# Two 64-token blocks of one expert done together, weight chunk by weight chunk, in the rare path of a mixture-of-experts kernel

## The reference, cut to what matters

```
def moe_ffn(h, ...):                       # h: 256 x 1024, 32 experts, the best 4 of each token
    top_v, top_i = lax.top_k(logits, 4); gates = softmax(top_v)
    # for each expert e and the tokens xb sent to it:
    u = xb @ w_mlp1[e] + b_mlp1[e]         # 1024 x 2048
    x_glu = minimum(u[..., ::2], 7); x_lin = clip(u[..., 1::2], -7, 7)
    a = x_glu * sigmoid(1.702 * x_glu) * (x_lin + 1)
    y = a @ w_mlp2[e] + b_mlp2[e]          # 1024 x 1024
    # each token: sum of gate * y over its 4 experts
```

## Time and profile before

| | us |
|---|---|
| median of 3 runs | 1716.1 (1715.84 to 1716.47) |
| the profiled execution | 1711.69 |
| its span, first to last instruction | 1709.9 |
| PE busy | 1612.0 (94%) |
| PE matmuls of the experts' first layer, usual path | 461.7 in 2048 records |
| PE matmuls of their second layer | 243.3 in 1088 records |
| DMA, mean over the span | 319 GB/s |

### The profile page before, as it was taken

The page is one execution under the profiler, slowest core; times in us unless marked ns, Lnnn a source line. Parts: engine busy times, 40 slices in busy tenths (PEclk is TensorE's granted clock), DMA queues, the critical chain, the costliest instruction groups (busy, mean ns, idle before and its releaser), DMA issues.

```text
span 1709.9 us, 18899 instructions
## 1 busy us (share of the span) xinstructions
PE 1612.0 (94%) x7649; PEld 911.7 (53%) x7650; DVE 584.0 (34%) x930; ACT 472.9 (28%) x810; POOL 120.8 (7%) x222
## 2 busy tenths in 40 slices
PE   4999988999999999789999999989999999999998
PEld 2767334343343323334344333327888887788886
DVE  2666111111111101111011110117664667666654
ACT  3543110010011101001011010116554565455543
POOL 2001110110111101010011100000000000000000
PEclk9999998899999999899999999999999999999999
DMA  8988992799999999969999999996555544455540
GB/s 331 408 324 337 382 425 112 316 427 427 426 427 426 428 426 428 401 252 426 427 427 427 426 427 427 427 427 236 189 181 195 174 148 148 197 195 187 176 169 25
DMA packets 76304, 545.58 MB, mean 319 GB/s; under 512 B 8592, under 2 KB 8976, under 8 KB 10528
## 3 DMA queue, kind: packets, MB, share of 16 engines
q1 hardware_dynamic: 75744, 542.95, 78.0%
q10 hardware_dynamic: 448, 1.11, 0.2%
HBM read 542.98 MB, written 1.05 MB: 318 GB/s over the span
## 4 chain that ended last, share of the span: by engine, by line
PE 78%; DMA 16%; DVE 2%; issue 1%; ACT 1%; PEldq 1%; POOL 0%; SPq 0%; DVEq 0%; POOLq 0%; ACTq 0%
PE bank L274 75%; DMA slot<-w_mlp 15%; PE bank L278 3%; DMA h<-x 1%; PEldq L86 0%; DMA slot<-w_in_tail 0%; POOL mg L284 0%; ACT sq L281 0%; DVE XL L284 0%; ACT whf L281 0%; DVE h L292 0%; DVE u_l L292 0%; DVE u_g L288 0%; DVE u_s L284 0%; DVE tmp L284 0%
## 5 line engine op out<-in xcount | busy, mean ns | idle before, releaser
L274 PE MATMUL bank<-slot,xt 128*64 128x512 f32 x2048 | 461.7, 605 | 20.0 <-DMA slot<-w_mlp 19.9
L274 PEld LDWEIGHTS bank<-slot,xt 128*64 128x64 f32 x2048 | 143.6, 139 | 321.5 <-issue 272.8
L274 PE MATMUL bank<-slot,at 128*64 128x512 f32 x1088 | 243.3, 600 | 2.9 <-ACT at L281 2.9
L274 PE MATMUL bank<-wht,XH 128*128 128x512 f32 x528 | 207.7, 398 | 2.5 <-DVE XL L284 1.5
L274 PE MATMUL bank<-wlt,XH 128*128 128x512 f32 x528 | 204.3, 392 | 0.0
L292 DVE SCALAR_TENSOR_TENSOR wlt<-slot,colt,wht 128x512 fp32r<-128x512 f32 x248 | 177.4, 760 | 78.8 <-ACT wht L281 78.6
L274 PE MATMUL bank<-wht,XL 128*128 128x512 f32 x528 | 204.0, 391 | 0.0
L281 ACT ACTIVATE wht<-slot,colt 128x512 fp32r<-128x512 f32 x248 | 164.4, 718 | 91.9 <-PE bank L274 91.9
L288 DVE TENSOR_SCALAR u_g<-bank 128x512 f32<-128x512 f32 x34 | 23.5, 692 | 470.1 <-PE bank L274 470.1
L274 PEld LDWEIGHTS bank<-slot,at 128*64 128x64 f32 x1088 | 77.3, 138 | 154.0 <-issue 154.0
L281 ACT ACTIVATE u_s<-u_g 128x512 f32<-128x512 f32 x34 | 21.4, 630 | 498.2 <-DVE u_g L288 498.2
(11 more groups left out here) (314 smaller groups left out, 1528.4 us busy)
## 6 DMA issues: line engine op xcount, KB each, us to landing
slot<-w_mlp SPq DMA_DIRECT2D x384, 1024.0 KB, 25.5
slot<-gu SPq DMA_DIRECT2D x44, 1024.0 KB, 4.8
slot<-w_ada SPq DMA_DIRECT2D x24, 1024.0 KB, 10.2
slot<-down SPq DMA_DIRECT2D x22, 1024.0 KB, 4.7
slot<-w_in SPq DMA_DIRECT2D x18, 1024.0 KB, 5.0
slot<-w_out SPq DMA_DIRECT2D x8, 1024.0 KB, 7.5
slot<-w_gate SPq DMA_DIRECT2D x8, 1024.0 KB, 4.8
slot<-w_br_a SPq DMA_DIRECT2D x2, 1024.0 KB, 4.8
```

What stands on the lines that cost most here:

```text
L274: return pe(lambda e: e.matmul(o, l, r, start=start, stop=stop), *after, **kw)
```

## The change

An expert with more than 64 tokens no longer does one block and then the usual code. It takes a body of its own that does both blocks and then goes back to behind the whole usual code of that expert; the usual code is what the others run in line. In that body `first` and `second` take a list of blocks (`parts`), go through the weights once, and alternate between the blocks every two matmuls; the last block's last matmul on a chunk releases it. The second block has banks of its own (`FX`, `FY`, those of the other parity). The two `swiglu`s follow each other, since they share `u_g`, `u_s` and `u_l`. The checks for more than 128 and 192 tokens now come first in the body. For odd experts the `beside` work comes at the end of the body. `first_weights` moves from inside expert 0 to behind it.

```
-def seldom(kind, queues, far_sems, ap, bound, tag, body):
+def seldom(queues, far_sems, ap, bound, tag, body):
...
+def either(queues, sems, far_sems, ap, bound, tag, near, far):
...
+        q.items.append(("either", tag, ap, bound, usual, path, s.h, s.n - n))
...
+        at_x = nc.alloc_sbuf_tensor_at("at_x", [128, 4, 128], F32, offset=place["xt_x"][0])
...
+        def first(e, parts, release):
+            for X, Y, sel_, _, t_sel_, _, _ in parts:
+                for g, bk in enumerate((X, Y)):
+                    mm(bank[bk][:, :], sel_, brow[:, 512 * g : 512 * g + 512], True, False, t_sel_, T["brow"], *free[bk])
+            steps = first_early(e, range(4))
+            for two in zip(steps[0::2], steps[1::2]):
+                for i, (X, Y, _, x_of, _, t_x_, s_) in enumerate(parts):
+                    for k, j in two:
...
+                        if j == 3 and release:
+                            end_ = {"sem": rel, "sig": last_}
...
+        def gather_far(e, n, b0, *after):
...
             for b in range(2):
-                t = tr(bank[2][0:64, b * 128 : b * 128 + 128], ow_x[:, b, :], t_w, *free[2], sig=b == 1)
+                t = tr(bank[b0][0:64, b * 128 : b * 128 + 128], ow_x[:, b, :], t_w, *free[b0], sig=b == 1)
...
+        def meet():
+            done = [q.now() for q in ways] + [(s_, s_.n) for s_ in far_sems]
+            for q in ways:
+                q.wait(done)
...
-            def more():
-                pe.wait([act_done, dve_done])
-                overflow(e, 1)
-                for n in (2, 3):
-                    seldom("skip", ways, far_sems, at_e, 64 * n, f"{e}_{n}", lambda n=n: overflow(e, n))
...
+            def far_first():
+                for n in (2, 3):
+                    seldom(ways, far_sems, at_e, 64 * n, f"{e}_{n}", lambda n=n: overflow(e, n))
+                return gather_far(e, 1, FX)
+
+            def far():
+                meet()
+                far_pe = far_sems[0]
+                t_x_, t_s_, t_w = aside(far_first)
+                (t_x, t_fx), t = first(e, [mine, (FX, FY, selt_x[:, :], lambda k: xt_x[:, k, :], t_s_, t_x_, far_pe)], True)
+                t_a = swiglu(X, Y, t_x, t)
+                if s_ == 0:
+                    beside[0]()
+                bias_2(Y, sel_)
+                t_at, t_l = transposed(X, at[:, :, :], t_a)
+                if s_ == 0:
+                    beside[1]()
+
+                def more():
+                    t_a = swiglu(FX, FY, t_fx, t, t_l)
+                    bias_2(FY, selt_x[:, :])
+                    return transposed(FX, at_x[:, :, :], t_a)[0]
+
+                t_fat = aside(more)
+                t = second(e, [(Y, at, t_at, None), (FY, at_x, t_fat, far_pe)], True)
+                out_of(Y, y, t)
+                aside(lambda: scatter_far(t_w, out_of(FY, y_x, t)))
+                if s_:
+                    beside[0]()
+                    beside[1]()
+                meet()
+
+            either(ways, [pe.sem, act.sem, dve.sem, rel], far_sems, at_e, 64, f"{e}", near, far)
...
-            t_even = expert(2 * p, [lambda b=b: scatter(p - 1, False, [b]) for b in range(2)] if p else [nothing, first_weights])
+            t_even = expert(2 * p, [lambda b=b: scatter(p - 1, False, [b]) for b in range(2)] if p else [nothing] * 2)
             if p == 0:
+                first_weights()
```

More of the change, by code:

```diff
@@ L1262, in first_early @@
             return [(k, q) for k in range(n) for q in qs] + [(k, q) for i in (0, 2) for k in range(n, 8) for q in qs[i : i + 2]]
[L1264 to L1277, removed]
-            return t_x, t
@@ L1280, in second @@
[L1280 to L1286, removed]
+        def first(e, parts, release):
[3 more added lines that the diff above has]
+            steps = first_early(e, range(4))
+            t_x = [None] * len(parts)
+            for two in zip(steps[0::2], steps[1::2]):
+                for i, (X, Y, _, x_of, _, t_x_, s_) in enumerate(parts):
+                    for k, j in two:
+                        c = c_w1[e][k]
+                        bk, h_ = (X, Y)[j // 2], j % 2
+                        last_ = i == len(parts) - 1
+                        if j == 3 and release:
+                            end_ = {"sem": rel, "sig": last_}
+                        else:
+                            end_ = {"sem": s_, "sig": k == 7 and (j == 1 or j == 3 and last_)}
+                        t = mm(bank[bk][64 * h_ : 64 * h_ + 64, :], x_of(k), buf(c)[:, 512 * j : 512 * j + 512], False,
+                               k == 7, landed(c), t_x_[k], **end_)
+                        if j == 1:
+                            t_x[i] = t
+                        if j == 3 and release:
+                            chunks[c]["done"] = t
+            return t_x, t
@@ L1287, in second @@
+        def second(e, parts, release):
             for k in range(8):
                 c = c_w2[e][k // 2]
[L1289 to L1293, removed]
+                for i, (Y, a_, t_at, s_) in enumerate(parts):
+                    last_ = i == len(parts) - 1
+                    for g in range(2):
+                        o = (k % 2) * D + 512 * g
+                        if k % 2 and g and release:
+                            end_ = {"sem": rel, "sig": last_}
+                        else:
+                            end_ = {"sem": s_, "sig": last_ and k == 7 and g == 1}
+                        t = mm(bank[Y][64 * g : 64 * g + 64, :], a_[:, k % 4, 64 * (k // 4) : 64 * (k // 4) + 64],
+                               buf(c)[:, o : o + 512], False, k == 7, landed(c), t_at, **end_)
@@ L1299, in second, with aside @@
             return [t1, t2]
-        nothing = lambda: None
-        def overflow(e, n):
+        ways = [pe, act, dve]
+        def aside(fn):
+            held = [q.sem for q in ways]
+            for q, s_ in zip(ways, far_sems):
+                q.sem = s_
+            out_ = fn()
+            for q, s_ in zip(ways, held):
+                q.sem = s_
+            return out_
+        def gather_far(e, n, b0, *after):
             for b in range(2):
                 t_o = ts(dve, oh_x[:, b, :], iota[:, 64 * n : 64 * n + 64], pos[:, b, e : e + 1], ALU.is_equal,
-                         pe.now(), s2=nscale[b], op1=ALU.mult)
+                         *after, pe.now(), s2=nscale[b], op1=ALU.mult)
             t_s_ = cp(dve, selt_x[:, :].rearrange("p (h j) -> p h j", h=2),
@@ L1323, in overflow @@
                            sig=b * g)
-            for q in (pe, act, dve):
-                q.wait([act.now(), dve.now(), pe.now()])
+        def meet():
+            done = [q.now() for q in ways] + [(s_, s_.n) for s_ in far_sems]
+            for q in ways:
+                q.wait(done)
+        def overflow(e, n):
+            t_x_, t_s_, t_w = gather_far(e, n, 0)
+            (t_x,), t_y = first(e, [(0, 1, selt_x[:, :], lambda k: xt_x[:, k, :], t_s_, t_x_, None)], False)
+            t_a = swiglu(0, 1, t_x, t_y)
+            bias_2(1, selt_x[:, :])
+            t_at, _ = transposed(0, at_x[:, :, :], t_a)
+            t_y = out_of(1, y_x, second(e, [(1, at_x, t_at, None)], False))
+            scatter_far(t_w, t_y)
+            meet()
             free[0:4] = [[] for _ in range(4)]
@@ L1343, in expert @@
[L1343 to L1346, removed]
+            sel_ = selt[i][s_][:, :]
+            mine = (X, Y, sel_, lambda k: xt[:, k, 64 * s_ : 64 * s_ + 64], t_selt[i], t_xt[i], None)
+            y = ypair[64 * s_ : 64 * s_ + 64, :]
```

63 lines of the change are left out of this document (47 added, 16 removed).

## The result

| | median us (lowest to highest) | profiled execution | its span |
|---|---|---|---|
| before, 5 runs | 1715.84 (1709.71 to 1716.47) | 1711.69 | 1709.9 |
| after, 5 runs | 1728.54 (1727.42 to 1728.93) | 1728.93 | 1726.9 |

The account below looks back on a forecast made before the run. The weights' DMA bounds the layer, through its last departure from 19 full slots. Path terms summed to 91.3 us, giving +5.5 at expert 3 and +4.35 at expert 17: +9.9 on the median, 1726 us, range 1716.5 to 1733.

Parts of the forecast that it names:

- main step: Expert layer: its end follows when the DMA last leaves the 19 full slots and at which chunk, not its idle time.
- the wall: Weight loads: all 19 slots full, so the DMA stops until a chunk is released.
- branch to the gather: Far body's entry: two checks ahead of the gather, 12.9 us, where before it took 6.45 and 7.64.
- gather to the first layer: Far body: 11.0 us, before 9.4, with a wait for DVE's copies and the other block's bias matmuls.
- activations: Far body between the layers: the two blocks' activations follow each other, 6.35 us with nothing beside them.
- rival 4: Slower, 13 in 100: TensorE at half clock between the layers and a way out of 4.24 us, 1735 us.
- Way out: Far body's end: jump over the expert's usual code, 1.4 us, middle of held and not held; count load, branches, semaphores 1.15.
- Expert 0: Turn of `ow` moved behind expert 0's second layer: 1.15 us, which delays expert 3.
- Waits for weights: TensorE in the expert layer: to stay near 20 us, less where TensorE itself has fallen back.
- break-even: Next expert's first release must come within 86.95 us of expert 2's end, 86.45 at expert 17, for a gain.
- Rivals 1 to 3: Faster: early release pays, 1696 us, 5 in 100; cheap checks, 1708.5 us, 5 in 100; third is rival 3.
- rival 3: No change, 15 in 100: second code packet asked for early and way out held, 1718.8 or 1716.5 us.

Follow-up runs that it names:

- experiment 3: The kernel after, but the far body releases its first layer's eight chunks together, with the last matmul: 1727.18 us, ratio to before 1.0071.
- experiment 7: The kernel before with the far path limited to 256 tokens, so tokens beyond 64 of experts 3 and 17 are left out: 1651.55 us.
- experiment 6: The kernel after with the third and fourth block's code out of line and the first copies back beside expert 0: 1713.37 us.
- experiment 1: The kernel after without the checks for over 128 and 192 tokens and the blocks they guard: 1710.34 us, ratio to before 0.9978.
- experiment 4: The kernel before with only the two checks moved ahead of the overflow block: 1715.02 us, ratio to before 1.0002.
- experiment 5: The kernel before with the third and fourth block's code behind all far code, so checks fall through: 1706.24 us, ratio to before 0.9951.

## Why the prediction was right, point by point

Its main step holds: the DMA's last departure from the wall sets the layer's end, and what is released earlier inside the body doesn't move it (experiment 3). But the forecast set this against the DMA's idle time, and expected less of that "in sum than 42 us". It was 48.7 at expert 3 and 26.6 at expert 17, and experiment 7 gives back just the idle time. The two are one measure: a later last departure is more idle time. The path, measured in after's profile:

| term | forecast | expert 3 | expert 17 |
|---|---|---|---|
| branch to the gather | 12.9 | 13.6 | 15.7 |
| gather to the first layer | 11.0 | 10.6 | 10.6 |
| first layer | 29.5 | 28.8 | 29.2 |
| activations | 6.35 | 6.95 | 6.95 |
| second layer | 14.05 | 16.0 | 16.2 |
| copies | 1.6 | 1.6 | 1.6 |
| scatter, next gather, way out | 11.2 | 10.2 | 10.2 |
| next expert's first chunk | 4.7 | 4.1 | 4.0 |
| sum | 91.3 | 91.9 | 94.4 |

- *Entry.* 0.7 us short at expert 3, 2.8 at expert 17. The forecast had the first check end 7.3 us behind the expert before. It did at expert 3; at 17 it took 6.53 us and ended at 9.3. The gather came 7.2 and 8.1 us later than in before, at or beyond the 4 to 7 that were to show it.
- *Between the layers.* I had written rival 4's fall to half clock as 13 in 100. It came at both experts: the window 315 to 322 of after has 0.51, and the second layers took 1.9 and 2.1 us more. The clock fell while PE stood: its transposes ended at 313.2, the window 313 to 315 still has 1.00, and 315 to 316 has 0.56. I should have put it in the sum.
- *Way out.* I took the middle of held and not held, 1.4; the jump took 0.29 us both times. By the Trainium skill's rule ("Runtime: NRT & Kernel Launch", "Instruction fetch mechanics") a target outside the two-page window waits for a fetch; these two jumps don't show it, as the earlier trace rows didn't. (The same section gives TensorE's instruction memory 128 KiB, eight packets of 16; code left that few packets ago may still be held there. No run here isolates it.) The profile names POOL's `ow` for the wait of 2.45 us, but it is the way out itself: DVE's last copies end 1.1 us behind PE (343.19 to 344.28), PE's jump starts at 344.5 and takes 0.29, its load of the count starts at 344.9 and its branch at 345.2, and the matmul starts at 345.64. That matmul does not read `ow`, and for the same wait in experiment 6 at expert 17 the profile names PE's sequencer. So the terms for copies, loads and branches held, and the 1.0 us by which the whole was too long is the jump.
- *Expert 0.* 1.0 us, forecast 1.15, seen at expert 2.
- *Waits for weights.* They were to stay near 20 us. They fell from 19.9 to 14.3. The forecast allowed for less only where TensorE itself had fallen back, and here it had, by the longer paths.
- *The break-even.* By my 86.95 and 86.45 us, these paths and expert 0's 1.0 give +5.9 and +7.9, in all 13.9; the trace has +4.0 at expert 16 (its second layer starts 507.86 us behind expert 0's first matmul, before 503.85) and 10.4 at the end. So against this profile of before the break-even was 1.9 and 1.5 us too early. Experiment 1 says the same: paths of 85.2 and 84.0 us and expert 0's term should give -3.1, the layer has -6.2. The same gap is in experiment 4 (first releases 2.4 and 0.7 us later, layer 0.4 longer) and experiment 5 (10.7 us earlier, layer 13.0 shorter). It is in no comparison that leaves before out: after and experiment 1 differ by 17.0 in their paths and 16.7 in the layer, experiments 6 and 5 by 9.9 and 10.1. So it lies with before: the layer of its one profile is 2.3 to 3.4 us longer than its paths say. The lag from release to DMA, 2.5 in the forecast, was about 2 in after and 2.3 and 3.1 in before; the rest I can't place.

In sum: +4.0 from the paths and expert 0 and -3.4 from the break-even, each a miss, left the 9.9 near the measured 10.4. That much of the closeness is luck. The medians' 12.7 us lies between the 10.4 of the layer and the 13.9 of the paths; the interval of the ratio goes from 11.1 to 17.3, and the router's 5 to 7 us, which one profile has and the next hasn't, lie over it. Rivals 1 to 3 fell: no check was cheap, and no release inside the body paid. Of rival 3 the cheap way out came true, of rival 4 the half clock; the one took back half of the other.

Which part costs what, by the layer: free of dear checks the two forms take 971.6 us (experiment 5) and 978.4 (experiment 1), so 6.8 of the 10.4 us are the interleaving; the checks cost 13.0 us where before has them and 16.7 where after has them, which is the other 3.7. By the medians of each set the checks cost 10.0 us in before and about 16 in after, which makes the second part about 6. Experiment 6, whose checks fall through but are still there, puts the interleaving at 10.1 by the layer and 7.1 by the medians. So 7 to 10 us are the interleaved path with its idle stretches, and what is left, at most some 6, is the move of the checks, which in before's own form measured 0.4 to 1 (experiment 4).

## What to carry to other kernels

When a ring of buffers stands full during a rare slow stretch, price the stretch by when the producer leaves the full ring for the last time; freeing buffers earlier inside it bought nothing here. Lay code so that the case that happens falls through: a check that steps over a body cost 2.8 to 6.8 us here in most cases, one that falls through 0.06 to 0.08. And when a wait is moved, count what stood behind it at both places, the engine's clock too: moving the checks alone changed nothing, taking the jump out of them gave 10 us.

## What the runs showed of the hardware

- Branches on PE into the far code and over a body at its head took 4.7 to 6.8 us while the DMA moved weights at about 420 GB/s; the second check at the old place took 2.8 and 4.2 with an idle DMA, the first 0.4. The jump back out of the far code took 0.18 to 0.43 us in every kernel that has one, whatever had been fetched since.
- Straight code seems to starve too: 3.53 us in the midst of a gather, behind three dear branches (experiment 4), with a packet on q8 2 us before it went on. The DMA was still busy there. This was seen once.
- TensorE ran at 0.50 of its clock after it had stood for 6.11 us at the exit in before (window 303 to 308), and at 0.51 between the layers in after (window 315 to 322), where the clock fell about 1.9 us into a stand of 2.85. Behind exits of 0.29 and 1.57 us at expert 3 (experiments 4 and 5) it ran at 1.00, but behind 1.64 us at expert 17 of experiment 5 it fell inside the layer (0.69 and 0.74 in the windows 732 to 738).
- In the router the clock was halved in six of nine profiles and whole in three, for the same instructions, and this moved everything behind it by 5 to 7 us: as much as the effect that was to be measured.
